# The second in-projection as five seven-product pairs, with a new order of its blocks

## The reference

```python
def second_block(x, positions, w_in, q_norm_g, w_uq, kv_norm_g, w_ukv, pool_w, pool_scale, w_out, ln_g, ln_b):
    h = x @ w_in                    # 1024 -> 512 + 256 + 64 + 512 + 512 + 512 columns
    x_q, x_kv, k_rope_raw, gate_a, u_pool, gate_b = jnp.split(h, splits, axis=-1)
    y_a = mla_branch(x_q, x_kv, k_rope_raw, positions, ...) * jax.nn.silu(gate_a)
    y_b = pool_branch(u_pool, pool_w, pool_scale) * jax.nn.silu(gate_b)
    mix = jnp.concatenate([y_a, y_b], axis=-1) @ w_out
    return layer_norm(alpha * x + mix, ln_g, ln_b)
```

## Time and profile before

| | us |
|---|---|
| median of three runs | 1684.82 |
| the profiled execution | 1683.6 |
| its span, first to last instruction | 1681.8 |
| PE busy in the span | 1666.5 |
| DVE, ACT, POOL busy | 1256.2, 795.6, 452.0 |
| second in-projection from its first free block on (1175.7 to 1382.1) | 206.4 |

### The profile page before, as it was taken

The page is one execution under the profiler, slowest core; times in us unless marked ns, Lnnn a source line. Parts: engine busy times, 40 slices in busy tenths (PEclk is TensorE's granted clock), DMA queues, the critical chain, the costliest instruction groups (busy, mean ns, idle before and its releaser), DMA issues.

```text
span 1681.8 us, 20879 instructions
## 1 busy us (share of the span) xinstructions
PE 1666.5 (99%) x7597; PEld 1373.9 (82%) x7597; DVE 1256.2 (75%) x1494; ACT 795.6 (47%) x1066; POOL 452.0 (27%) x270
## 2 busy tenths in 40 slices
PE   9999999999999999999999999999999999999998
PEld 7788788888787888888888888888888888788786
DVE  6478791369999888888888879889737936777654
ACT  5667741236854433444344444455332327566531
POOL 4223222100015654555454000005432442201000
PEclk9999999999999999999999999999999999999999
DMA  7111112053412232222322974762322221010351
GB/s 265 52 48 37 50 51 76 25 213 94 169 51 88 76 98 75 75 87 84 91 75 96 327 267 153 247 195 62 101 88 63 88 88 31 26 63 26 114 218 75
DMA packets 161098, 176.99 MB, mean 105 GB/s; under 512 B 13566, under 2 KB 114692, under 8 KB 161028
## 3 DMA queue, kind: packets, MB, share of 16 engines
q1 hardware_dynamic: 158708, 167.67, 30.7%
q10 hardware_dynamic: 2320, 8.39, 1.3%
HBM read 140.38 MB, written 35.65 MB: 105 GB/s over the span
## 4 chain that ended last, share of the span: by engine, by line
PE 93%; DVE 4%; ACT 1%; issue 1%; DMA 1%; DVEq 0%; SPq 0%; ACTq 0%
PE ps L962 31%; PE ps L2603 27%; PE ps L2557 19%; PE ps L2849 5%; PE ps L2834 3%; PE ps L2499 1%; PE ps L2685 1%; PE ps L2888 1%; PE ps L2806 1%; DVE pt_lo L2376 1%; PE ps L2523 1%; DVE prob L2333 1%; PE ps L2822 1%; DMA x_tok<-in_x 1%; ACT pt_hi L1646 0%
## 5 line engine op out<-in xcount | busy, mean ns | idle before, releaser
L985 POOL TENSOR_TENSOR w_lo<-w_raw,w_hi 128x1024 fp32r<-128x1024 f32 x52 | 138.0, 2654 | 594.1 <-ACT w_hi L1097 592.3
L2603 PE MATMUL ps<-hop_hi_P,wop_hi_P 128*128 128x512 f32 x672 | 263.6, 392 | 2.0 <-DVE u L1974 0.8
L2603 PE MATMUL ps<-hop_lo_P,wop_hi_P 128*128 128x512 f32 x672 | 262.9, 391 | 0.0
L2603 PE MATMUL ps<-hop_hi_P,wop_lo_P 128*128 128x512 f32 x672 | 262.8, 391 | 0.0
L991 POOL TENSOR_TENSOR wop_lo_P<-pair_sum,wop_hi_P 128x512 fp32r<-128x512 f32 x90 | 137.3, 1526 | 351.5 <-ACT wop_hi_P L1108 351.5
L962 PE MATMUL ps<-h_hi,w_hi 128*128 128x512 f32 x688 | 214.1, 392 | 0.0
L962 PE MATMUL ps<-h_lo,w_hi 128*128 128x512 f32 x688 | 211.9, 389 | 0.0
L962 PE MATMUL ps<-h_hi,w_lo 128*128 128x512 f32 x688 | 211.8, 389 | 0.0
L962 PEld LDWEIGHTS ps<-h_hi,w_hi 128*128 128x128 f32 x688 | 128.2, 188 | 30.0 <-issue 4.3
L2603 PEld LDWEIGHTS ps<-hop_hi_P,wop_hi_P 128*128 128x128 f32 x672 | 126.9, 189 | 30.5 <-DVE u L1974 1.6
L962 PEld LDWEIGHTS ps<-h_lo,w_hi 128*128 128x128 f32 x688 | 129.1, 188 | 27.1
(11 more groups left out here) (386 smaller groups left out, 3403.8 us busy)
## 6 DMA issues: line engine op xcount, KB each, us to landing
pair_raw<-in_w_up SPq DMA_DIRECT2D x48, 512.0 KB, 4.9
w_raw<-in_w_in SPq DMA_DIRECT2D x46, 512.0 KB, 3.9
dn_raw<-gu_park SPq DMA_DIRECT2D x84, 256.0 KB, 3.9
dn_raw<-in_w_down SPq DMA_DIRECT2D x60, 256.0 KB, 3.1
gu_park<-up_cv SPq DMA_DIRECT2D x24, 512.0 KB, 2.6
out_raw<-in_w_out SPq DMA_DIRECT2D x30, 256.0 KB, 2.8
x_tok<-in_x SPq DMA_DIRECT2D x4, 1024.0 KB, 8.1
x_park<-xs SPq DMA_DIRECT2D x1, 4096.0 KB, 13.2
```

The costliest lines, as they stand in the source:

```text
L985: nc.gpsimd.tensor_tensor(lo[:, :], raw[:, :], hi[:, :].bitcast(f32), ALU.subtract).then_inc(w_lo_done, 1)
L2603: mm = nc.tensor.matmul(dst, w[q][:, k, :], x[q][:, k, :], start=a, stop=b, skip_group_check=True)
```

## The change

Ten of the 19 column blocks (two of kv, four of q, four of the attention's gate) are done as five pairs with seven products each, kv first, then q, then the gates. The nine others (pool values and gates, key rope) stay as they are and come first. Each k-half of x times token half needs sums and differences (`mix_sum`, 8 DVE instructions of 1024 columns), and these have high and low parts of their own. The sine and cosine arguments are computed on a quarter of the columns with the tokens spread over the partitions, written to HBM and read back. The scaled key-rope tile goes to HBM and back too. Residual tiles, pooled results and gates get other buffers.

```diff
-N_POOL = N_IN2 + Q_TILES + KV_TILES
-N_GATE = N_POOL + 2 * len(WINDOWS)
-N_KR = N_GATE + HEADS
+N_POOL = N_IN2
+N_KR = N_POOL + 2 * len(WINDOWS)
...
+        IN_PAIRS = 5
+        IN_COLS = ((4 * P, 5 * P), (0, P), (2 * P, 3 * P), (832, 832 + P), (832 + 2 * P, 832 + 3 * P))
+        IN_RUN = ("P1", "P6", "P5", "P2", "P7")
+        IN_ORDER = [(q, 0) for q in IN_RUN]
+        for n in range(IN_PAIRS - 1):
+            after = IN_RUN[1:] if n + 2 < IN_PAIRS else ("P6", "P5", "P7", "P2")
+            IN_ORDER += [("P1", n + 1), ("P4", n), ("P3", n)] + [(q, n + 1) for q in after]
+        IN_ORDER += [("P4", IN_PAIRS - 1), ("P3", IN_PAIRS - 1)]
...
+        def in_bank(n, name):
+            first, second = ps[2 * ((n + 1) % 2)], ps[2 * ((n + 1) % 2) + 1]
+            if n == IN_PAIRS - 1:
+                first, second = second, first
...
```

```diff
+            for n in range(IN_PAIRS):
+                if n == 0:
+                    sp.wait_ge(block_done, N_KR)
+                for f in range(2):
+                    if n >= 1:
+                        sp.wait_ge(pair_sum_done, 4 * PAIRS + 4 * n)
+                        sp.wait_ge(wop_lo_done, in_made(("P2", "P4")[f], n - 1))
+                    sp.dma_start(in_raw[f][:, :, :], w2_v[:, :, IN_COLS[n][f]:IN_COLS[n][f] + P]).then_inc(pair_in[f], 16)
+            sp.wait_ge(wop_lo_done, in_made("P3", IN_PAIRS - 1))
+            sp.wait_ge(product, in_run("P5", IN_PAIRS - 1))
```

PE's order of the blocks and a product:

```diff
+            block_with(N_POOL + 2, ps[0], lambda: (pe.wait_ge(final_gain, 16), pe.wait_ge(gb_done, 1), by_token(0)))
+            by_token(1)
+            pe.wait_ge(rstd3_spread, 1)
+            block_with(N_POOL + 3, ps[1], lambda: (by_token(2), pool_product(0)))
+            by_token(3)
+            pe.wait_ge(u_done, 2)
+            block_with(N_POOL + 4, ps[0], lambda: by_token(4))
...
+            block_with(N_POOL + 7, ps[1], lambda: pool_product(2))
+            pe.wait_ge(u_done, 4)
+            block_with(N_KR, ps[0], lambda: pool_product(3))
...
+                for k in range(4):
+                    x_hi, x_lo = ix_parts(q, slice(k, k + 1))
+                    for w, x, a, b in ((in_hi[q], x_hi, q in ("P1", "P6", "P5") and k == 0, False), (in_hi[q], x_lo, False, False),
+                                       (in_lo[q], x_hi, False, k == 3)):
+                        mm = nc.tensor.matmul(dst, w[:, k, :], x[:, 0, :], start=a, stop=b, skip_group_check=True)
...
             def free_slot(j):
                 if j == 0:
+                    pe.wait_ge(ga_done, 1)
+                elif j == 1:
+                    pe.wait_ge(ga_done, 3)
+                elif j == 2:
                     pe.wait_ge(ga_done, 4)
...
-            pe.wait_ge(latn_lo_d, 3)
-            pe.wait_ge(latn_lo_p, 3)
+            pe.wait_ge(latn_lo_d, 2)
+            pe.wait_ge(latn_lo_p, 2)
```

DVE's order, whose queue feeds most of PE's waits:

```diff
+            pooled(0)
+            pool_gate(0)
+            pool_weight(0)
+            trig()
+            mix_sum("P5")
+            pooled(1)
...
+            pool_gate(2, "P6")
+            mix_sum("P4")
+            mix_low("P7")
+            mix_low("P6")
+            pooled(3)
+            pool_weight(3)
+            pooled_gate(2)
+            pool_gate(3)
+            in_weight_sums(0)
+            pooled_gate(3)
+            mix_low("P4")
...
+            for n in range(IN_PAIRS):
+                in_third_sums(n)
+                if n == 2:
+                    latent_factor(0, T2)
+                elif n == 3:
+                    latent_factor(1, T1)
+                    latent_factor(1, T2)
+                    latent_normed(0)
+                    latent_normed(1)
+                    in_second_sum(4)
+                elif n == 4:
+                    latent_low(0)
+                    latent_low(2)
+                    gate2(1)
+                    gate2(0)
+                in_result(n, 1)
+                if n == 4:
+                    gate2(3)
+                in_result(n, 0)
+                if n + 2 < IN_PAIRS:
+                    in_second_sum(n + 1)
+                if n == 1:
+                    latent_factor(0, T1)
+                elif n == 2:
+                    latent_normed(4)
+                    latent_normed(5)
+                elif n == 3:
+                    latent_normed(2)
+                    latent_normed(3)
+                if n + 2 < IN_PAIRS:
+                    in_weight_sums(n + 2)
...
```

Inside `pooled(0)` the first gate's scaling stands ahead of the pooled difference; `pool_gate` waits for the tanh and multiplies. `latent_factor` is a reciprocal over half a tile, `in_result` adds the last product and scales by `rstd3`, `gate2` multiplies an attention gate by one plus its tanh. `rotate(0)` follows the loop and has `gate2(2)` behind its sum. ACT's end of the stage:

```diff
+                if n == 3:
+                    latent_high(2)
+                    latent_high(3)
+                    act.wait_ge(wop_lo_done, in_made("P3", IN_PAIRS - 1))
+                    high(N_UQ)
+                    park_gate(1)
+                    park_gate(0)
...
+                if n == 4:
+                    act.wait_ge(pos_in, POS_BACK)
+                    act.wait_ge(sums_done, in_sums("C22", n))
+                    swap_halves(0, kr_raw)
...
+            act.wait_ge(product, in_run("P5", IN_PAIRS - 1))
+            act.wait_ge(latn_done, Q_TILES + KV_TILES)
+            high(N_UQ + 1)
+            park_gate(3)
+            act.wait_ge(rope_v, 1)
+            nc.scalar.copy(kr_hi[:, :], scr[2][:, :]).then_inc(rope_hi, 1)
+            park_gate(2)
```

More of the change, by code:

```diff
@@ L634, in _, with lat_made @@
+        def lat_made(i):
+            return LATS.index(i) + 1
         @block.sync
@@ L1055, in _ @@
                                         ALU.subtract).then_inc(pl_lo, 1)
[L1056 to L1064 removed]
+            low(N_POOL + 2)
@@ new lines, in _, with in_low @@
+            low(N_POOL + 3)
+            for g in range(len(WINDOWS)):
+                pooled_low(g)
+                for n in (N_POOL + 2 * g + 4, N_POOL + 2 * g + 5):
+                    if n <= N_KR:
+                        low(n)
+            def in_low(q, n):
+                pool.wait_ge(wop_hi_done, in_made(q, n))
+                nc.gpsimd.tensor_tensor(in_lo[q][:, :, :], in_weight(q), in_hi[q][:, :, :].bitcast(f32),
+                                        ALU.subtract).then_inc(wop_lo_done, 1)
@@ new lines, in _ @@
+            for q in IN_FIRST:
+                in_low(q, 0)
+            for n in range(-1, IN_PAIRS):
+                last = n + 1 == IN_PAIRS
+                if not last:
+                    in_low("P7", n + 1)
+                    in_low("P4", n + 1)
+                if 0 <= n < 3:
+                    add_latent(PAIR_LATS[n][1])
+                if n == 3:
+                    latent_low(1)
+                if not last:
+                    in_low("P3", n + 1)
+                if 0 <= n < 3:
+                    add_latent(PAIR_LATS[n][0])
+                for q in IN_NEXT:
+                    if n + 2 < IN_PAIRS:
+                        in_low(q, n + 2)
+                if n == 3:
+                    latent_low(3)
+                    pool.wait_ge(product, in_run("P6", IN_PAIRS - 1))
+                    low(N_UQ)
@@ L1066, in _ @@
+            pool.wait_ge(gate_parked[1], GATE + 16)
+            low(N_UQ + 1)
+            low(N_UQ + 2)
+            latent_low(5)
+            for n in range(N_UQ + 3, N_BLOCKS):
+                low(n)
             pool.wait_ge(block_done, N_BLOCKS - 1)
@@ L1578, in _ @@
-            gate(1)
-            gate(2)
-            gate(3)
-            for q in range(2):
-                act.wait_ge(gate_parked[q], GATE + 16 * HEADS // 2)
             swapped = (scr[1], scr[3], scr[1])
@@ new lines, in next_high, with pooled_high, pool_tanh @@
+            def next_high(n):
+                act.wait_ge(block_done, read(n - 2))
+                high(n)
+            def pooled_high(g):
+                if g >= 1:
+                    act.wait_ge(pool_mm, g)
+                else:
+                    act.wait_ge(pw_in, 16)
+                nc.scalar.copy(pw_hi[:, :], pw_raw[:, g, :]).then_inc(pw_hi_done, 1)
+                act.wait_ge(pl_done, g + 1)
+                nc.scalar.copy(pooled_hi[:, :], scr[3][:, :]).then_inc(pl_hi, 1)
+            def pool_tanh(g):
+                act.wait_ge(gb_scaled, g + 1)
+                if g >= 2:
+                    act.wait_ge(y_parked, 16 * (g - 1))
+                nc.scalar.activation(y_pool[:, g % 2, :], ps[3 if g == 0 else 1][:, :], ACT.Tanh, scale=0.5).then_inc(th_done, 1)
@@ new lines, in latent_high @@
+            def latent_high(i):
+                if i < Q_TILES:
+                    act.wait_ge(latn_done, KV_TILES + i + 1)
+                if i == 0:
+                    act.wait_ge(product, in_run("P6", IN_PAIRS - 1))
+                elif i == Q_TILES:
+                    act.wait_ge(ga_scaled, HEADS)
+                    act.wait_ge(gate_parked[1], GATE + 16 * HEADS // 2)
+                nc.scalar.copy(latents()[i][0], lat_tile(i)).then_inc(latn_hi, 1)
+            next_high(N_POOL + 2)
```

693 lines of the change are left out of this document (461 added, 232 removed).

## The result

| kernel | time, us | runs | against before | profiled span | mean granted clock |
|---|---|---|---|---|---|
| before | 1685.14 (1683.40 to 1685.79) | 6 | | 1681.8 | 0.997 |
| changed | 1690.90 (1688.93 to 1692.59) | 6 | 1.0036 (1.0023 to 1.0049) | 1688.0 | 0.993 |

A forecast was written before the change was run, and what follows sets the result against it. TensorE (PE), busy 99% of the span, was taken as the bound: 13.6 - 4.3 - 0.3 - 3.3 - 0.7 = 5.0 us less, 1678.6 against the profiled run, 1679.8 against the median; range 1674 to 1687.

The forecast's parts named there:

- PE work, 13.6 us less: Second in-projection: five pairs of 84 matmuls in place of 96 remove 60 matmuls at 0.2267 us each, 13.6 us.
- The head's first gate, 4.3 us: Third pool block: PE's token transposes wait for the first gate's product, delayed by DVE meeting POOL's low part; cost 4.3 us.
- the other case, 2.1 with DVE in first: Head's first gate: if DVE's pooled difference gets in before POOL's low part, no meeting, and the wait costs 2.1 us.
- The head's rest and the pairs, 0.3 and 0: Rest of the head up to the first product: 0.3 us of 0 to 3; waits within the pairs: 0.
- The third sum, 0.3: Last pair: DVE's third sum ends at -5.1 us, needed at -5.4, so PE waits 0.3 us.
- Tail, 3.3: Last pair into q-up projection: meetings of DVE's and POOL's low parts delay slots 0 and three; cost 3.3 us.
- the case priced at 3.5: Tail: if POOL goes next instead of DVE, PE starts the q-up projection at 3.5 us instead of 2.4.
- that case had 5.6: Tail in the other order, POOL ahead of DVE: cost 5.6 us instead of 3.3.
- Slot seven, 0.7 of 0 to 2.5: Q-up slot seven: added casts and low parts fall within the ropes, the low parts mostly hidden; cost 0.7, of 0 to 2.5.
- The clock, nothing in the sum and one rival at 0.05: Whole stretch: granted clock taken as 1.00, no cost in the sum; a fall only in rival 4, chance 0.05.
- a fall of the clock behind the gate's wait: Head: the prediction called itself wrong if the clock falls behind the first gate's wait of about 4 us.
- rival 4: Clock falls at the head's wait: one block at 1.2 GHz takes 10.9 us more; 5.9 more in all, 1690.7; chance 0.05.

The follow-up runs named there:

- experiment 3: Changed kernel with the token transposes half a block later and the third pool gate ahead of a difference of the activations: 1687.65 us, ratio 1.0023.
- experiment 5: Changed kernel with the two gate products that free slots 0 and 1 issued on DVE ahead of query latent low parts 0 and 2: 1691.64 us, ratio 1.0046.
- experiment 1: Changed kernel with 18 dummy matmuls on PE ahead of its head wait for the first gate's product: 1689.2 us, ratio 1.0033.
- 8: Changed kernel with the edits of experiments 7, 6 and 4 together: 1677.16 us, ratio 0.9957.
- experiment 9: Experiment 8's kernel with P6's low parts between the last gate's scaling and product, and the last pool gate ahead of the weight sums: 1676.52 us, ratio 0.9951.
- 7: Experiment 3's kernel with the sixth product's low parts moved behind the fourth pool window and weight on DVE: 1687.64 us, ratio 1.0019.
- 6: Experiment 5's kernel with the first q-up weights loaded, cast and split earlier, and the second block's cast ahead of the key swap: 1687.63 us, ratio 1.0023.
- 4: Changed kernel with the high and low parts of the first two q-up tiles made between the rotations, not behind both: 1684.28 us, ratio 0.9998.
- experiment 2: Changed kernel with 9 dummy matmuls, in place of experiment 1's 18, ahead of PE's head wait: 1690.94 us, ratio 1.0036.
- experiment 11: Changed kernel with the second product run ahead of the seventh in the last pair, undoing that part of the change: 1690.33 us, ratio 1.0036.

## Why the prediction was wrong

- **PE work, 13.6 us less: right.** 60 matmuls fewer, slot 0.227.
- **The head's first gate, 4.3 us: right in size and tile (y_pool), and partly by luck.** The text took POOL's subtraction to start ahead of DVE's pooled difference and to hold it. In the trace DVE was first: the difference took its 1.22 us and POOL's subtraction 3.47 in place of 2.4. What POOL then held was DVE's next instruction, the edge correction of one column, 2.23 us where its like takes 0.17 (15 columns, in experiment 3):

```profile
1182.18 1.22 DVE L2496 SCALAR_TENSOR_TENSOR scr<-scr,scr 128x1024 f32<-128x1024 f32 x1
1183.43 2.23 DVE L2501 TENSOR_TENSOR small<-scr,rc 128x1 f32<-128x1 f32 x1
1182.18 3.47 POOL L1109 TENSOR_TENSOR w_lo<-w_raw,w_hi 128x1024 fp32r<-128x1024 f32 x1 [3.05 <-ACT w_hi L1259]
```

  Either way DVE is through just after POOL, at 1185.7. So the other case, 2.1 with DVE in first, didn't exist: it forgot the edge correction behind the difference. The terms as written also add up to 1190.6, so 4.2.
- **The head's rest and the pairs, 0.3 and 0: right.** No wait from 1199 to 1369 us.
- **The third sum, 0.3: right** (0.4).
- **Tail, 3.3: the order was the other one.** The text left open whether DVE or POOL is next in the fight for slot 0, 0.1 us apart, and took DVE. POOL started the weights' low part at 1373.29, 0.3 ahead of DVE's second part, and DVE's second ended 1.1 behind it:

```profile
1373.29 2.62 POOL L1109 TENSOR_TENSOR w_lo<-w_raw,w_hi 128x1024 fp32r<-128x1024 f32 x1 [0.70 <-ACT w_hi L1259]
```

  DVE's two low parts took 6.72 us in the changed kernel and 4.54 in experiment 5, where they start behind the gates:

```profile
1370.28 6.72 DVE L2631 TENSOR_TENSOR qn_lo<-lat,qn_hi 128x1024 fp32r<-128x1024 f32 x2
```

```profile
1372.46 4.54 DVE L2631 TENSOR_TENSOR qn_lo<-lat,qn_hi 128x1024 fp32r<-128x1024 f32 x2
```

  So slot 0 came at 1378.27, 3.0 us behind the last product (1375.26): the case priced at 3.5. Slot three came at 1391.57, so 16.3 against 10.9, 5.4 late, where that case had 5.6. But 1.7 of this is PE running slowly, not waiting: the waits of the tail, 0.4, 2.85 and 0.5, add up to 3.8, near the 3.3 of the sum. That is luck, as the slow matmuls behind slot 0 hid 1.4 us of the wait at slot three: with the clock kept in experiment 1 it was 1.9 and not 0.5.
- **Slot seven, 0.7 of 0 to 2.5: this step failed.** It waited 4.7. I had written that the low parts which are new within the ropes hide "mostly". DVE's timeline, first of the changed kernel, then of the one before, shows what they lengthen:

```profile
1405.49 1.23 DVE L2701 TENSOR_TENSOR scr<-ps,cos_t 128x1024 f32<-128x1024 f32 x1
1406.63 2.18 DVE L2705 SCALAR_TENSOR_TENSOR scr<-scr,sign,sin_t 128x1024 f32<-128x1024 f32 x1
1408.84 3.41 DVE L2711 TENSOR_TENSOR scr<-scr,scr 128x1024 f32<-128x1024 f32 x1
...
1416.94 1.22 DVE L2728 TENSOR_TENSOR qh_lo<-ps,qh_hi 128x1024 fp32r<-128x1024 f32 x1
```

```profile
1404.76 1.22 DVE L2285 TENSOR_TENSOR scr<-scr,sin_t 128x1024 f32<-128x1024 f32 x1
1406.01 1.23 DVE L2287 TENSOR_TENSOR scr<-scr,scr 128x1024 f32<-128x1024 f32 x1
```

  The rotation's multiply and add meet POOL's low parts of kvn (1405.05) and of the weights (1408.77) and take 5.6 us where they took 2.5. That is 3.1. The rotation also starts 1.9 us later (1405.49 against 1403.62) and PE comes 0.9 earlier (1413.6 against 1414.5); less the 1.4 that the bank was early before, that makes 4.5. I priced the added instructions, and not the instructions that they lengthen on the one chain that frees the bank.
- **The clock, nothing in the sum and one rival at 0.05: this step failed too, and it is the larger one.** Every stretch that I had read was without waits, so I gave the clock a single case in which one whole block runs at 1.2 GHz. The trace of before had a price in it, further up. The clock falls twice there, behind runs of one-column matmuls (L2616) and without a wait, and the falls cost 1.6 and 1.7 us (4.00 x 0.40, 8.00 x 0.21):

```profile
468.00:472.00 4.00, 4.00 (x12) 3.09 (x12) 4.00 (x5) 4.00 (x7) 0.00 (x0) 0.60 0.00 0
476.00:484.00 8.00, 8.00 (x46) 7.05 (x46) 6.58 (x11) 5.08 (x7) 0.00 (x0) 0.79 0.00 0
```

  What happened is smaller and came more than once: a fall behind each of the three long waits, 1.85 + 1.7 + 2.38 = 5.9 us. The sum should have carried about 2 us for each wait of some microseconds that it put on PE, beside the wait itself. With that alone, on the waits of the head and the tail as forecast, it would have been 1.0 us less, not 5.0. The prediction had named a fall of the clock behind the gate's wait as a sign of being wrong, and its sum went by 1.00 all the same.
- Put together: -13.6 + 4.3 + 0.4 + 2.85 + 0.5 + 4.7 + 5.9 + 1.0 = +6.05, where the last term is what was left over.

The price that I gave rival 4, 1690.7, is close to what came, by an accident of two errors: one block at half clock for three partial falls, and 8.6 us of waits for 12.8.

That the waits and the clock behind them are the cause is shown by experiments 8 and 9, which take them away by order alone and turn +5.8 us into -7.0 and -7.5. What a single fix brings is less than its wait and the clock behind it (over the stretch 4.8 of 6.2, 3.1 of 5.1 and 6.1 of 7.1 us in 7, 6 and 4). In 7 and 6 a part comes back as a longer wait further on; in 4 the fall behind the head's unchanged wait cost more, 2.6 us for 1.85. All three together brought about the sum of what they brought singly, with 4.3 us of waits left. The share of the clock by itself is read from the traces and from one comparison of spans (experiment 1), not from a run in which it alone was changed.

## What to carry to other kernels

Where TensorE is full, taking matmuls out turns the spare time of every helper engine into a term of the sum: look at each instruction that frees a bank, list what stands ahead of it on its engine, and move first what nobody wants yet. Price a wait of TensorE of two microseconds and more at its length plus about two of slower matmuls until a run shows otherwise. Judge a fix by the waits that it moves as well as by its time: here three that gained 2.2, 2.9 and 6.4 us one by one gained 13.3 together, which is their sum within the noise, and two of them left longer waits elsewhere when made alone (0.5 became 2.9, 4.7 became 5.7).

## What the runs showed of the chip that I had not expected

The clock behind a wait. In all the traces of this study, the mean granted clock in the first 4 us behind each wait from 1150 to 1440 us:

| PE's wait | cases | at 1.00 | fell, to |
|---|---|---|---|
| 4.1 to 5.7 us | 15 | 0 | 15, to 0.50 to 0.61 |
| 2.2 to 3.1 us | 12 | 3 | 9, to 0.57 to 0.69 |
| 1.4 to 1.9 us | 5 | 5 | 0 |

So the loss doesn't grow in step with the wait: 2.2 us cost as much as 4.3 (experiment 2), and the same 2.8 us at slot 0, with the same instructions ahead of it, cost 1.7 us in the changed kernel and nothing in experiments 1 and 7. The 4.7 us at slot seven cost 2.4 us in the changed kernel (13.26 against 10.88), 1.9 in experiment 1 and 3.0 in experiment 2. What decides between these is left open by the runs. The Trainium skill (TensorE: Matmul & The Clock Gate, HAM oscillation) says that gaps between bursts of matmuls bring the clock down to half; that is what the first row shows, while in this stage of the kernel before, with no gap, it was 1.00 throughout. A gap isn't the only thing that brings it down: at 468 and 476 us it falls in the kernel before with PE busy all the time, behind one-column matmuls. These falls differ from one execution to the next with the same instructions: the mean from 464 to 492 us was 0.88 in most of the traces, 0.82 in experiment 9 and 0.94 in experiment 11.

A transfer that starts earlier can end another one later: in experiment 5 two parks of 512 KB moved up by 6 us and a read-back of eight parts of 128 KB beside them landed 2 us late (1384.35 against 1382.4 for the last part; one pair of traces), and slot three, three steps further on, came 1.9 us later than in the changed kernel (1393.46 against 1391.57), although slot 0 came 1.2 earlier.

The tanh table's load behaved as in the earlier trace rows: 1.28 us at 1186.96, and the tanh at 1188.25, 0.01 behind it.
